# Between attention and experts: low part of the first row tile by halves, its high part ahead of the sigmoid table, one first-row add on VectorE instead of GpSimd

## What is computed

```python
x = x + g1 * y                                    # y: attention output @ w_o
h = rms_norm(x, norm_ffn_g[i]) * (1.0 + sc2) + sh2
x = x + g2 * grouped_moe(h, router_w, router_bias, w_gate[i], w_up[i], w_down[i])

def grouped_moe(h, ...):
    scores = sigmoid(h @ router_w)                # 16 experts, in 4 groups of 4
    sel = scores + router_bias
    # the group with the largest sum of its two best; in it the two best experts
    out = sum over e of gates[:, e] * ((silu(h @ w_gate[e]) * (h @ w_up[e])) @ w_down[e])
```

## Time and profile before

| | us |
|---|---|
| median of 3 runs (lowest, highest) | 1154.24 (1153.57, 1154.55) |
| the profiled execution's own time | 1153.23 |
| its span, first to last instruction | 1151.3 |
| TensorE busy (matmul) | 1100.7 (96%) |
| VectorE busy | 603.7 (52%) |
| ACT busy | 423.7 (37%) |
| GpSimd busy | 101.0 (9%) |
| mean granted TensorE clock | 0.995 |

### The profile page before, as it was taken

One profiled execution on the slowest core, in us unless ns is written; L12 is line 12 of the kernel. 1 busy time (PEld: TensorE's weight loads), 2 busy tenths in 40 slices (PEclk: granted clock), 3 DMA queues, 4 the chain that ended last, 5 costly groups with the idle time before them and its releaser, 6 DMA issues.

```text
span 1151.3 us, 17400 instructions
## 1 busy us (share of the span) xinstructions
PE 1100.7 (96%) x6870; PEld 744.2 (65%) x6870; DVE 603.7 (52%) x1164; ACT 423.7 (37%) x731; POOL 101.0 (9%) x193
## 2 busy tenths in 40 slices
PE   9999999999999999999999999987999999999986
PEld 9887667899999967777634434326888754343422
DVE  3588756767887765676423322327756522332223
ACT  6445434644444444474401202106547412020200
POOL 0211123111121120020000000002000100000000
PEclk9999999999999999999999999998999999999999
DMA  9987684997999878665899999996576789999995
GB/s 289 299 254 275 219 319 143 262 341 216 329 332 305 259 257 308 208 232 175 335 399 409 409 409 408 410 402 221 176 264 239 281 300 409 409 409 409 409 409 232
DMA packets 164910, 356.14 MB, mean 309 GB/s; under 512 B 10840, under 2 KB 79704, under 8 KB 164704
## 3 DMA queue, kind: packets, MB, share of 16 engines
q1 hardware_dynamic: 147792, 295.81, 71.0%
q0 software_dynamic: 17024, 59.26, 15.0%
q10 hardware_dynamic: 16, 0.02, 0.0%
HBM read 351.89 MB, written 7.36 MB: 312 GB/s over the span
## 4 chain that ended last, share of the span: by engine, by line
PE 77%; DMA 9%; DVE 7%; ACT 3%; SPq 2%; issue 1%; POOL 0%; POOLq 0%; DVEq 0%; ACTq 0%
PE bank L632 38%; PE bank L1230 15%; PE bank L1240 8%; DMA ering<-in_moe_w_up 3%; DMA work<-in_moe_w_up 3%; PE bank L1199 3%; PE bank L557 2%; DMA ering<-in_ada_w 1%; PE bank L803 1%; PE bank L937 1%; SPq L502 1%; DVE wlo L622 1%; PE bank L2020 1%; PE bank L1303 1%; PE bank L968 1%
## 5 line engine op out<-in xcount | busy, mean ns | idle before, releaser
L622 DVE TENSOR_TENSOR wlo<-wraw,whi 128x1024 fp32r<-128x1024 f32 x150 | 179.1, 1221 | 58.3 <-ACT whi L618 57.6
L618 ACT ACTIVATE whi<-wraw 128x1024 fp32r<-128x1024 f32 x150 | 153.8, 1052 | 57.1 <-PE bank L632 51.7
L632 PE MATMUL bank<-a_hi,whi 128*128 128x256 f32 x512 | 146.3, 286 | 0.4 <-DVE wlo L622 0.3
L632 PE MATMUL bank<-a_lo,whi 128*128 128x256 f32 x512 | 144.8, 283 | 0.0
L632 PE MATMUL bank<-a_hi,wlo 128*128 128x256 f32 x512 | 144.8, 283 | 0.0
L1230 PE MATMUL bank<-ering,work 128*64 128x512 f32 x528 | 118.5, 595 | 6.0 <-DMA ering<-in_moe_w_gate 4.3
L1479 DVE TENSOR_TENSOR work<-work,bank 128x512 f32<-128x512 f32 x16 | 11.0, 687 | 197.7 <-PE bank L1230 197.7
L1368 ACT ACTIVATE o_hi<-work 128x512 fp32r<-128x512 f32 x32 | 20.2, 631 | 231.5 <-DVE work L1428 231.1
L632 PE MATMUL bank<-whi,a_hi 128*128 128x512 f32 x256 | 104.1, 407 | 0.8 <-DVE wlo L622 0.8
L632 PEld LDWEIGHTS bank<-a_hi,whi 128*128 128x128 f32 x512 | 98.0, 191 | 9.5 <-issue 7.3
L632 PE MATMUL bank<-whi,a_lo 128*128 128x512 f32 x256 | 99.9, 390 | 0.0
(11 more groups left out here) (349 smaller groups left out, 1931.4 us busy)
## 6 DMA issues: line engine op xcount, KB each, us to landing
ering<-in_moe_w_gate SPq DMA_DIRECT2D x36, 1024.0 KB, 18.5
ering<-in_moe_w_up SPq DMA_DIRECT2D x30, 1024.0 KB, 14.6
ering<-in_moe_w_down SPq DMA_DIRECT2D x30, 1024.0 KB, 18.4
work<-in_ada_w POOLq DMA_DIRECT2D x44, 512.0 KB, 7.5
ering<-in_ada_w POOLq DMA_DIRECT2D x38, 512.0 KB, 5.4
wraw<-in_w_in SPq DMA_DIRECT2D x28, 512.0 KB, 7.2
work<-in_moe_w_up SPq DMA_DIRECT2D x14, 1024.0 KB, 16.4
work<-in_moe_w_down SPq DMA_DIRECT2D x14, 1024.0 KB, 18.0
```

The source lines that it names most:

```text
L618: nc.scalar.activation(w_hi(c), wraw[:, c % RING, :], ACT.Copy).then_inc(w_hi_done, 1)
L622: nc.vector.tensor_tensor(w_lo(u[0]), wraw[:, u[0] % RING, :], w_hi(u[0]).bitcast(F32), ALU.subtract).then_inc(w_lo_done, 1)
L632: mm = nc.tensor.matmul(out_ap, l, r, start=first and n == 0, stop=last and n == len(terms) - 1)
```

## The change

- GpSimd adds only the first half of row tile 0. The second half is added by VectorE after its third multiplication, ahead of its first add of row tile 1. The adds of VectorE now signal `x_done` by 1, 1 and 2.
- ACT's square of row tile 0 waits for GpSimd's one add and for VectorE's first.
- ACT writes the high part of row tile 0 in two halves right after its copy of bank 3, ahead of the sigmoid's table load. The first half signals `rt_full_a`, the second `hn_done`.
- VectorE writes the low part of row tile 0 in two halves: the first between the inversion and its wait for the router's matmuls, the second between the copy to `strips` and its wait for the fold. The whole low part ahead of the choice is gone.
- The numbers of `busy` matmuls, row tile 1, the choice, the gather and all loads stay.

```diff
         def rows_added(l):
-            return 3 * SUB_POOL + 2 * (l + 1)
+            return 3 * SUB_POOL + l + 1
 
         def add_first_rows(pool, l):
 
-            for n in range(2):
-                cols = slice(n * HALF, (n + 1) * HALF)
-                pool.wait_ge(x_tmp, 4 * l + n + 1)
-                nc.gpsimd.tensor_tensor(x[:, 0, cols], x[:, 0, cols], hn[:, 0, cols], ALU.add).then_inc(sub_done, 1)
+            pool.wait_ge(x_tmp, 4 * l + 1)
+            nc.gpsimd.tensor_tensor(x[:, 0, 0:HALF], x[:, 0, 0:HALF], hn[:, 0, 0:HALF], ALU.add).then_inc(sub_done, 1)
...
                 if n in (4, 6) and t == 0:
                     act.wait_ge(sub_done, rows_added(n // 2 - 2))
+                    act.wait_ge(x_done, xs - X_W + 1)
...
+        def norm_halves_hi(act, n):
+
+            act.wait_ge(nrm_inv, n + 1)
+            for half, signal in ((0, rt_full_a), (1, hn_done)):
+                cols = slice(half * HALF, (half + 1) * HALF)
+                nc.scalar.activation(hn_hi[:, 0, cols], x[:, 0, cols], ACT.Copy, scale=sm[:, M_RS:M_RS + 1]).then_inc(signal, 1)
+
+        def norm_half_lo(dve, n, half):
+
+            if half == 0:
+                dve.wait_ge(rt_full_a, n - 2)
+            else:
+                dve.wait_ge(hn_done, 2 * n - 1)
+            cols = slice(half * HALF, (half + 1) * HALF)
+            nc.vector.scalar_tensor_tensor(out=hn_lo[:, 0, cols], in0=x[:, 0, cols], scalar=sm[:, M_RS:M_RS + 1],
+                                           in1=hn_hi[:, 0, cols].bitcast(F32), op0=ALU.mult, op1=ALU.subtract)
...
-                        pe.wait_ge(rt_full_a, l + 1)
+                        pe.wait_ge(rt_full_a, 2 * l + 1)
...
+                norm_halves_hi(act, 4 + 2 * l)
                 warm(ACT.Sigmoid)
-                norm_split_hi(act, 4 + 2 * l, 0)
...
-                    dve.wait_ge(x_tmp, 4 * count + n + 1)
-                    if n == 3:
-                        dve.wait_ge(sub_done, rows_added(count))
-                    nc.vector.tensor_tensor(x[:, t, cols], x[:, t, cols], hn[:, t, cols], ALU.add).then_inc(x_done, 2)
+                    for m in ((1, 2) if n == 2 else (3,)):
+                        at = slice((m % 2) * HALF, (m % 2 + 1) * HALF)
+                        dve.wait_ge(x_tmp, 4 * count + m + 1)
+                        if m == 3:
+                            dve.wait_ge(sub_done, rows_added(count))
+                        nc.vector.tensor_tensor(x[:, m // 2, at], x[:, m // 2, at], hn[:, m // 2, at], ALU.add
+                                                ).then_inc(x_done, 2 if m == 3 else 1)
...
                 norm_invert(dve, n + 1)
+                norm_half_lo(dve, n + 1, 0)
                 dve.wait_ge(rt_ps, 4 * l + 1)
                 nc.vector.tensor_copy(strips, psum[4][:, 0:S]).then_inc(rt_full, 1)
+                norm_half_lo(dve, n + 1, 1)
...
-                norm_split_lo(dve, n + 1, 0)
                 dve.wait_ge(rt_sig, l + 1)
```

## The result

The changed kernel takes 1152.0 us (median of 22 runs, 1150.68 to 1154.14) against 1153.66 (22 runs, 1151.92 to 1155.49) for the kernel before: ratio 0.9986, 95% interval 0.9980 to 0.9993, so 1.6 us less, between 0.8 and 2.3. The direction was forecast, with a gain of 0.8 us; the lower end of the stated range, 1152.2 to 1154.7, lies 0.2 us above the measured median. A second set of runs of the same changed kernel gave 0.9992 (0.9983 to 1.0001), 0.9 us.

A forecast was written before the change was run, and what follows sets the result against it. The expert stage was taken as bound by its weight stream, whose start follows the gather, held by unused matmuls. 0.41 us in each of two layers, 0.8 in all, takes the median from 1154.24 to 1153.4 us; range 1152.2 to 1154.7.

The forecast's parts named there:

- What bounds the kernel, and that the stream hands gains on: Expert stage ends when its last weights land; the DMA hole, over 2 us per layer, passes on an earlier gather.
- Rival D: Weight stream: bound from its first load on, so its start does not follow and nothing is gained, 1154.2 us; 5%.
- The unused matmuls as the gate: TensorE before the ranks: 36 unused records still end at 558.37, so the ranks start at 558.13, only 0.41 us earlier.
- Rival A: Ranks: VectorE's chain alone sets them, not the unused matmuls; 0.80 us per layer, 1.6 in all, 1152.6 us; 7%.
- The sign that the prediction named: Ranks start some 0.2 us before the unused matmuls end, without wait, and VectorE idles before them.
- the term of 0.41 us per layer: Ranks and gather start 0.41 us earlier in each of two layers, 0.8 in all, none given back later.
- part 1: Add moved from GpSimd to VectorE: 0.2 to 0.25 us earlier for TensorE and ACT, up to 0.5 if undisturbed.
- the 0.12 us (new add undisturbed): Copy to `strips`: starts 0.12 us earlier if GpSimd does not disturb VectorE's new add, in all 1.1 us.
- the 0.37 us (turn): What TensorE could win at the turn of `x` at best; with the mask's 0.80, 1.17 per layer, 2.3 in all.
- Parts 2 and 3: ACT's high halves, 0.72 us each, cost nothing ahead of the table load; VectorE's low halves, 0.75 each, fill waits.
- Rival C: ACT's sigmoid comes late behind the moved table load; with a 1.28 us drain 0.4 us lost in all, 1154.7; 8%.
- Rival B: VectorE's first low half holds up the strips by 0.95 us; 0.5 per layer lost, 1155.3; 15%, mostly 1153.8 to 1154.5.

The follow-up runs named there:

- 26 calls: Changed kernel with 26 instead of 18 unused matmul calls ahead of the ranks: 1156.18 us, ratio 1.0027 against the kernel before.
- only the add: Kernel before plus only the second first-row add moved from GpSimd to VectorE, the norm parts unchanged: ratio 0.9998 against the kernel before.
- the changed kernel with 14 calls: Changed kernel with 14 instead of 18 unused matmul calls ahead of the ranks: 1151.29 us, ratio 0.9984 against the kernel before.
- only the halves: Kernel before plus only the high and low parts by halves, GpSimd still doing both first-row adds: ratio 1.0001 against the kernel before.
- the version with 14 and 4 calls: Changed kernel with 14 instead of 18 unused matmul calls ahead of the ranks and 4 instead of 6 ahead of the gather: 1151.31 us, ratio 0.9973.
- profiled executions with 14 calls: Kernel before with 14 instead of 18 unused matmul calls ahead of the ranks, profiled twice: ratio 1.0007; the second execution 1156.31 us.

## Why the prediction was off

**What bounds the kernel, and that the stream hands gains on: right.** The 26 calls cost 3.1 us where the stage grew by 2.6, the version with both sets of unused matmuls shorter gained 3.1 where the stage gained 2.6, and the first load that waits is issued 0.51 us earlier in each layer. Rival D is out. One row was misread on the way: the 18.19 us of the earlier trace rows are the load's own time on the chain, not a wait of TensorE. TensorE waited 0.63 us for it:

```profile
732.34 1.94 PE L1230 MATMUL bank<-ering,work 128*64 128x512 f32 x8 [0.63 <-DMA ering<-in_moe_w_up]
```

The conclusion drawn from it, that the stage ends when its last weights have landed, stands: the last product of the stream waits for its load in each of the 28 streams (0.61 or 0.62 us).

**The unused matmuls as the gate: right.** The forecast start of the ranks, 558.13 or 13.02 after the first multiplication, was met: 13.02. Rival A (1152.6) has nearly the measured time, but not the mechanism: with A the ranks would start on the mask, and the mask waited 0.5 us. The sign that the prediction named, idle time of VectorE before the ranks, is not in the trace in this form, since VectorE had the low part of row tile 1 to do; the gap between the mask's end (12.50) and the ranks' start (13.02) is the sign.

**The ranks' start was met by two errors that cancel.** The fold was forecast to stay at its place and moved 0.08 us ahead; the ranks were to start 0.24 us ahead of the unused matmuls' end, as the gather does, and start 0.16 ahead.

**The step that failed in the sum, the term of 0.41 us per layer: the stage measured 0.51.** The ranks moved by the forecast 0.41, the gather by 0.51. Two places. First, "The gather follows 2.48 us after the ranks": it follows 2.38 after. In the 2.48 of the earlier trace rows lay the first weight load of the ranks (PEld), which TensorE did not do ahead while it waited. In the changed kernel that load starts 0.11 us ahead of its matmul (558.72 and 558.83); before, both start together:

```profile
558.54 0.30 PEld L2252 LDWEIGHTS bank<-sm,con 128*128 128x128 f32 x2 [0.36 <-DVE sm L3009]
```

It is so in all variants: where the ranks wait for the mask the gather follows 2.47 or 2.48 after them (before; only the add, 13.17 to 15.65; the changed kernel with 14 calls, 12.56 to 15.03), where they do not wait, 2.37 or 2.38 (only the halves; 26 calls). With both low halves behind the copy to `strips`, where mask and unused matmuls end nearly together, it is 2.48 too. The wait that went took 0.1 us more with it than its own length. Second, part 1, the new add: it was taken as starting when GpSimd's ends. It started at once, 1.80 after the first multiplication, beside GpSimd's, and was stretched from 0.69 to 0.80. So it ended at 2.60 instead of 2.74, the last add started 0.05 earlier than before and not 0.05 later, and the inversion behind the copies of VectorE came 0.15 earlier ("stays", said the prediction). Of these 0.15 us the add explains 0.05; the copies also followed the last add more closely, 0.61 us after its start instead of 0.70, for which the trace names no cause. The low half then began 0.12 us after the end of the high half and not 0.04, so 0.08 was left for the fold. The nearest row, 0.96 us, was the wrong neighbour: there VectorE ran beside two operations of GpSimd, here beside the end of one.

The bounds had an error of their own: the 0.12 us (new add undisturbed) and the 0.37 us (turn) that the sum uses are not worked out anywhere, and part 1 has up to 0.5 for the same thing.

**Parts 2 and 3: right.** A high half takes 0.71 us (0.72 forecast), a low half 0.75. The table load follows the halves without a gap and takes 1.28, and the sigmoid is released by the logits. Rival C is out, and with it the drain of about 1380 ns that the Trainium skill (ScalarE: Activation LUTs, What ACT_TABLE_LOAD costs) puts at every switch, for this trace: between the end of the second high half (552.29 + 1.33 = 553.62) and the table load at 553.65 lie 0.03 us. Rival B's mechanism is real, at 0.2 us per layer and not 0.5; the copy to `strips` is later than before (8.22 against 8.05) only where the halves come without the add. The Trainium skill's lock (SBUF — State Buffer, SBUF: two separate sides) would have had the add blocked for the rest of GpSimd's instruction; it was stretched by 0.11 while 0.25 of GpSimd's add were left (547.61 against 546.58 + 1.28 = 547.86), so the trace agrees that the two get in each other's way and not with a block to the end.

**The level and the range.** The anchor was 1154.24, a median of three runs; over 22 it is 1153.66, and 1153.1 to 1153.9 in later sets. That is 0.6 us of the 1.4 between 1153.4 and 1152.0. The forecast gain was 0.2 short of the stage's, and the last 0.6 is the difference between the stage's 1.0 and the measured 1.6 of that set, which the second set did not show. The range allowed 0.5 us to each side for the spread, and then put its lower end on A with the anchor as it stood; it took the three runs' median as if it were exact. So two things failed, of which the level weighs more: with 1153.66 as anchor the same range would have been 1151.6 to 1154.1 and would have held 1152.0, while the stage's true 0.51 with the old anchor gives 1153.2. What of the last 0.6 us belongs to the change and what to the measurement stays open: intervals of 0.7 to 1.0 us to either side cannot tell it.

## What to carry to other kernels

Where an engine runs a fixed list of filler (matmuls that nobody uses), a gain on the engines that feed it is worth at most what the filler leaves; move or shorten the filler with it, as the version with 14 and 4 calls did (stage 17.00 instead of 17.81), and look at the granted clock over many executions when doing so. Work put into a wait is free only if it is over when the wait ends, and the first low half ended 0.2 us late. For changes this small, marks inside the stage, counted from its first instruction, repeat to 0.01 us where the total does not to 0.5.

## What the hardware showed unexpectedly

- The granted clock fell to half level after TensorE had begun to work again, not in the idle time: in one execution idle 558 to 559, clock 1.00 until 560, 0.50 from 561 to 563. By the estimates above it fell 1.4 us after TensorE had begun again in one execution and 2.3 us in the other. The same 1.1 us of idle time was followed by a fall in the first layer in both profiled executions with 14 calls and in neither in the second layer; 2 us was followed by none in the profiled execution, while half of that kernel's runs have a lower mean clock and a longer time. What decides it stays open.
- Two engines that get in each other's way may stretch rather than queue: VectorE's add 0.80 instead of 0.69 us in the changed kernel, with GpSimd's own add at the 1.28 of the earlier trace rows, where before GpSimd's second took 1.79 beside an add of VectorE that kept its 0.69.
- From the first expert product to the last load waited for, a layer takes 199.06 to 200.48 us from execution to execution: 1.4 us of spread over a stretch in most of which the DMA engines move 409 GB/s, more than the stage gains in both layers.
